# One attention stage of an encoder kernel: score matmuls of two heads interleaved, separate banks for transposed probabilities, rotation split anew over the engines, row factors spread by transposes

## The reference

```python
def rms_norm(x, g):
    x32 = x.astype(jnp.float32)
    y = x32 * lax.rsqrt(jnp.mean(x32 * x32, axis=-1, keepdims=True) + NORM_EPS)
    return (y * g.astype(jnp.float32)).astype(x.dtype)

def apply_rope(x, cos, sin):
    x1, x2 = jnp.split(x, 2, axis=-1)
    return jnp.concatenate([x1 * c - x2 * s, x2 * c + x1 * s], axis=-1)

# mixer of layer 0
q, k, v = jnp.split(h @ w_in, [1024, 1152], axis=-1)      # 16 heads of q, 2 of k, 2 of v
q = apply_rope(q...); k = apply_rope(k...)
logits = einsum('bnqhgd,bnkhd->bnhgqk', qc, kb) * 64 ** -0.5   # chunk n: 64 queries, 128 keys
logits = where(valid, logits, -inf)
probs = softmax(concatenate([logits, sink]))[..., :-1]
out = einsum('bnhgqk,bnkhd->bqhgd', probs, vb) @ w_out
```

## Time and profile before

| what | value |
|---|---|
| median of 3 runs | 1840.58 us (1840.41 to 1841.6) |
| profiled execution | 1839.91 us, span 1838.1 us |
| busy: PE, PEld, DVE, ACT, POOL | 1808.4, 1479.7, 914.1, 623.0, 148.8 us |
| granted TensorE clock, mean | 0.999 |
| first attention, first scores to last transposes | 410.0 to 484.0 us from the span's start |

### The profile page before, as it was taken

How to read it: one execution, slowest core, us unless ns; L and a number is a source line. 1 busy time by engine, 2 the same in 40 slices (tenths; PEclk the granted TensorE clock), 3 DMA queues, 4 the chain that set the end, 5 groups by cost and what they waited for, 6 DMA issues and landing times.

```text
span 1838.1 us, 23399 instructions
## 1 busy us (share of the span) xinstructions
PE 1808.4 (98%) x8601; PEld 1479.7 (80%) x8601; DVE 914.1 (50%) x1407; ACT 623.0 (34%) x1044; POOL 148.8 (8%) x124
## 2 busy tenths in 40 slices
PE   7999999999999999999999999999999999999998
PEld 5888888877788888888888888888766788888886
DVE  5443433468654434335543343456897544344344
ACT  5422222335543223223322222233466442222222
POOL 0100100012101001000110010100000010010010
PEclk9999999999999999999999999999999999999999
DMA  6333333233233333332333333234111333333321
GB/s 173 109 95 99 92 103 89 83 106 84 76 97 95 100 92 102 97 92 86 103 103 94 98 94 103 83 94 113 30 40 58 92 102 101 95 91 103 92 83 55
DMA packets 322097, 169.94 MB, mean 92 GB/s; under 512 B 13362, under 2 KB 317679, under 8 KB 322031
## 3 DMA queue, kind: packets, MB, share of 16 engines
q1 hardware_dynamic: 321680, 168.26, 32.0%
q10 hardware_dynamic: 350, 0.83, 0.1%
HBM read 162.50 MB, written 2.10 MB: 90 GB/s over the span
## 4 chain that ended last, share of the span: by engine, by line
PE 64%; issue 29%; DVE 3%; DMA 2%; POOL 1%; SPq 1%; ACT 0%; POOLq 0%; DVEq 0%; ACTq 0%
PE bank L1077 21%; PE bank L1078 21%; PE bank L1079 21%; POOL work L458 1%; DVE work L934 1%; DMA w_raw<-b_kvup 1%; SPq L388 0%; DMA r_kv<-work 0%; DMA work<-x 0%; PE bank L1195 0%; PE bank L1105 0%; DVE w_lo L710 0%; PE bank L1182 0%; PE bank L1094 0%; DMA m_q<-work 0%
## 5 line engine op out<-in xcount | busy, mean ns | idle before, releaser
L1077 PE MATMUL bank<-h_hi,w_hi 128*128 128x512 f32 x1536 | 601.2, 391 | 1.9 <-issue 1.7
L1079 PE MATMUL bank<-h_hi,w_lo 128*128 128x512 f32 x1536 | 598.3, 390 | 0.0
L1078 PE MATMUL bank<-h_lo,w_hi 128*128 128x512 f32 x1536 | 598.2, 389 | 0.0
L710 DVE TENSOR_TENSOR w_lo<-w_raw,w_hi 128x1024 fp32r<-128x1024 f32 (+2 forms) x320 | 394.4, 1233 | 317.1 <-ACT w_hi L518 309.0
L518 ACT ACTIVATE w_hi<-w_raw 128x1024 fp32r<-128x1024 f32 (+2 forms) x320 | 319.5, 998 | 296.1 <-PE bank L1079 296.0
L1077 PEld LDWEIGHTS bank<-h_hi,w_hi 128*128 128x128 f32 x1536 | 288.8, 188 | 62.3 <-issue 2.2
L1079 PEld LDWEIGHTS bank<-h_hi,w_lo 128*128 128x128 f32 x1536 | 288.6, 188 | 60.3
L1078 PEld LDWEIGHTS bank<-h_lo,w_hi 128*128 128x128 f32 x1536 | 288.9, 188 | 59.1
L1077 PE MATMUL bank<-y_hi,w_hi 128*128 128x512 f32 x832 | 325.1, 391 | 0.9 <-DVE xT L782 0.7
L1079 PE MATMUL bank<-y_hi,w_lo 128*128 128x512 f32 x832 | 323.8, 389 | 0.0
L1078 PE MATMUL bank<-y_lo,w_hi 128*128 128x512 f32 x832 | 323.7, 389 | 0.0
(11 more groups left out here) (136 smaller groups left out, 972.7 us busy)
## 6 DMA issues: line engine op xcount, KB each, us to landing
w_raw<-ffn_gu SPq DMA_DIRECT2D x176, 512.0 KB, 3.8
w_raw<-ffn_d SPq DMA_DIRECT2D x64, 512.0 KB, 3.7
w_raw<-ffn_d SPq DMA_DIRECT2D x32, 384.0 KB, 3.3
w_raw<-a_in SPq DMA_DIRECT2D x10, 512.0 KB, 3.9
w_raw<-a_out SPq DMA_DIRECT2D x8, 512.0 KB, 3.7
w_raw<-b_out SPq DMA_DIRECT2D x8, 512.0 KB, 3.6
w_raw<-b_in SPq DMA_DIRECT2D x5, 512.0 KB, 3.9
w_raw<-b_qup SPq DMA_DIRECT2D x16, 144.0 KB, 2.3
```

Of the source, the lines that this page charges most:

```text
L710: last = v.tensor_tensor(w_lo[:, sl, 0:k, 0:m], w_raw[:, sl, 0:k, 0:m], w_hi[:, sl, 0:k, 0:m].bitcast(F32), ALU.subtract)
L1077: t.matmul(b[:, :], wh, hi[:, c, :], start=c == 0, stop=False)
L1078: t.matmul(b[:, :], wh, lo[:, c, :], start=False, stop=False)
L1079: last = t.matmul(b[:, :], wl, hi[:, c, :], start=False, stop=c == k - 1)
```

## The change

Four things change, three of them in the first attention.

1. `scores_a`: the loop over chunks is outside and the loop over the two heads inside, so that consecutive matmuls address the four 64 by 64 quarters of the array. Both heads' `s_full` come with the last chunk. The transposed probabilities go to banks 5 and 6 (`TA`); the scores wait for the exponentials of the pair before (`exp_done`), and the transposes for ACT's copy of the pair before.
2. The query block is copied from its bank by ACT without scaling (`raw`); the norm's factors are multiplied into the cosine and sine tables once, by DVE. ACT makes this copy between its two copies of transposed probabilities (ahead of everything else at pair 0).
3. From block 2 on, SP issues two of the four exchange DMAs and ACT the other two, after its second copy and before `high`. SP's exchanges from block 2 on stand one weight load earlier. POOL makes only the cosine product; the sum is made by DVE (`rotated`) right after `sine_a`. DVE's `low` comes after the probabilities.
4. `diag` is gone. PE transposes the column of factors, read 128 times over, with the identity: four transposes instead of four products with ones. It waits for the last of the four short steps only.

```diff
@@ sync, exchange
+        def exchange(eng, n, c, parts):
+            eng.wait_ge(evac_done, block_a(n, c) + FIRST + 1)
+            if c >= 2:
+                eng.wait_ge(rot_done, c - 1)
+            for x in parts:
+                y = x ^ 1
+                eng.dma_start(swapped[c % 2][x * ROPE_B:(x + 1) * ROPE_B, :],
+                              raw_a[y * ROPE_B:(y + 1) * ROPE_B, c % 2, :]).then_inc(swap_in[c % 2], 16)
...
-                    sp.wait_ge(sine_done, c - 1)
-                for x in range(4):
...
+                exchange(sp, k_block, c, range(4) if c < 2 else (0, 1))
             for j in range(2, 2 + PAIRS + KD):
+                if 9 <= j < 8 + PAIRS:
+                    swap(j - 7)
                 if j < 2 + PAIRS:
                     load(k_block + j, 0, cols(a_in[0], (j - 2) * P, P))
...
-                elif 8 <= j < 8 + PAIRS:
-                    swap(j - 7)
+                elif j == 8:
+                    swap(1)
@@ gpsimd
                 g.tensor_tensor(dst, raw, cos, ALU.mult).then_inc(t1_done, 1)
+                if c >= 2:
+                    return
...
-            pool.wait_ge(t_in, 32)
+            pool.wait_ge(table_r, 2)
@@ scalar
-            for k in range(3):
-                high(n + k + AHEAD)
+            def raw(c):
+                blk = block_a(n, c)
+                act.wait_ge(pe_done, blk + FIRST + 1)
+                if c >= 2:
+                    act.wait_ge(rot_done, c - 1)
+                a.activation(raw_a[:, c % 2, :], bank[RING[blk][0]][:, :], ACT.Copy).then_inc(evac_done, 1)
+            high(n + AHEAD)
+            raw(0)
+            high(n + 1 + AHEAD)
+            act.wait_ge(evac_done, n + 1 + FIRST + 1)
+            high(n + 2 + AHEAD)
+            raw(1)
             for p in range(PAIRS + 1):
                 if p > 0:
                     for e in range(2):
                         act.wait_ge(t_full, 2 * (p - 1) + e + 1)
-                        a.activation(pt_a[:, e, :], SC[e][:, :], ACT.Copy).then_inc(pt_done, 1)
+                        a.activation(pt_a[:, e, :], TA[e][:, :], ACT.Copy).then_inc(pt_done, 1)
+                        if e == 0 and p + 1 < PAIRS:
+                            raw(2 + p)
+                elif p + 1 < PAIRS:
+                    raw(2 + p)
                 if p + 1 < PAIRS:
+                    exchange(act, n, 2 + p, (2, 3))
                     high(n + 3 + p + AHEAD)
@@ vector
-                if spread:
-                    for i in range(TT):
-                        last = v.tensor_scalar(diag[:, i, :], ident, st[:, 5, i:i + 1], None, ALU.mult)
-                    last.then_inc(diag_ready, 1)
...
-            def scaled_a(c):
...
+            def rotated(c):
+                dve.wait_ge(sine_done, c + 1)
+                dve.wait_ge(t1_done, c + 1)
+                q = qt_a[:, c % 2, :]
+                v.tensor_tensor(q, q, swapped[c % 2][:, :], ALU.add).then_inc(rot_done, 1)
...
+            v.tensor_tensor(cos_a, cos_a, r_x[:, :], ALU.mult).then_inc(table_r, 1)
+            v.tensor_tensor(sin_a, sin_a, r_x[:, :], ALU.mult).then_inc(table_r, 1)
...
-                if p + 1 < PAIRS:
-                    scaled_a(2 + p)
...
                 if p + 1 < PAIRS:
-                    low(n + 3 + p + AHEAD)
                     sine_a(2 + p)
+                    rotated(2 + p)
...
+                if p + 1 < PAIRS:
+                    low(n + 3 + p + AHEAD)
                 if p > 0:
                     pair_out(p - 1)
@@ tensor
-                pe.wait_ge(diag_ready, count["stat"])
+                pe.wait_ge(nstep, 4 * count["stat"])
...
-                    last = t.matmul(MISC[:, i * P:(i + 1) * P], ones[:, :], diag[:, i, :], start=True, stop=True)
+                    last = t.transpose(MISC[:, i * P:(i + 1) * P], st[:, 5, i:i + 1].to_broadcast([P, P]), ident)
...
+                    if p == 0:
+                        pe.wait_ge(v_ready, 1)
+                    else:
+                        pe.wait_ge(pt_done, 2 * (p - 1) + e + 1)
...
-                for e in range(2):
-                    if p > 0:
-                        pe.wait_ge(pt_done, 2 * (p - 1) + e + 1)
-                    rows = slice(e * HD, (e + 1) * HD)
-                    for c in range(NC):
+                if p > 0:
+                    pe.wait_ge(exp_done, 2 * p)
+                for c in range(NC):
+                    for e in range(2):
+                        rows = slice(e * HD, (e + 1) * HD)
```

More of the change, by code:

```diff
@@ L188, in build @@
         r_kv = sb("r_kv", [P, S])
-        diag = sb("diag", [P, TT, P])
         cst = sb("cst", [P, C_END])
@@ L238, in build @@
         VTB = bank[5:7]
+        TA = bank[5:7]
         OB = bank[7]
@@ L266, in build @@
         nstep = sem("nstep")
-        diag_ready = sem("diag_ready")
         silu_done = sem("silu_done")
@@ L274, in build @@
         t1_done = sem("t1_done")
+        table_r = sem("table_r")
         rot_done = sem("rot_done")
@@ L381, in swap @@
             def swap(c):
-                sp.wait_ge(evac_done, block_a(k_block, c) + FIRST + 1)
-                if c >= 2:
-                    sp.wait_ge(sine_done, c - 1)
-                for x in range(4):
-                    y = x ^ 1
-                    sp.dma_start(swapped[c % 2][x * ROPE_B:(x + 1) * ROPE_B, :],
-                                 raw_a[y * ROPE_B:(y + 1) * ROPE_B, c % 2, :]).then_inc(swap_in[c % 2], 16)
+                exchange(sp, k_block, c, range(4) if c < 2 else (0, 1))
             for j in range(2, 2 + PAIRS + KD):
+                if 9 <= j < 8 + PAIRS:
+                    swap(j - 7)
                 if j < 2 + PAIRS:
@@ L744, in refine, with rms_values @@
                 dve.wait_ge(nstep, count["n"])
-            def rms_values(m, width, spread=True, between=None):
+            def rms_values(m, width, between=None):
                 dve.wait_ge(misc_full, m + 1)
@@ L871, in _ @@
             n = ffn(0, 0, G_MIX)
-            def scaled_a(c):
-                b = product(block_a(n, c))
-                if c >= 2:
-                    dve.wait_ge(rot_done, c - 1)
-                v.tensor_tensor(raw_a[:, c % 2, :], b[:, :], r_x[:, :], ALU.mult).then_inc(evac_done, 1)
             def sine_a(c):
+                dve.wait_ge(table_r, 2)
                 dve.wait_ge(swap_in[c % 2], 64 * (c // 2 + 1))
@@ L889, in _ @@
             rms_spread(3, r_x)
-            scaled_a(0)
+            dve.wait_ge(t_in, 32)
+            v.tensor_tensor(cos_a, cos_a, r_x[:, :], ALU.mult).then_inc(table_r, 1)
+            v.tensor_tensor(sin_a, sin_a, r_x[:, :], ALU.mult).then_inc(table_r, 1)
             low(n + 1 + AHEAD)
             b = product(n + 1)
+            dve.wait_ge(evac_done, n + FIRST + 1)
             v.tensor_tensor(vpad[:, CHUNK:CHUNK + S], b[:, :], r_x[:, :], ALU.mult).then_inc(evac_done, 1)
             low(n + 2 + AHEAD)
-            dve.wait_ge(t_in, 32)
-            scaled_a(1)
             sine_a(0)
@@ L1049, in _ @@
             n = ffn(n, M_F, G_FIN, keep=True)
-            rms_values(M_F + 2, D, spread=False)
+            rms_values(M_F + 2, D)
             for i in range(TT):
@@ L1180, in transposes_a @@
                     pe.wait_ge(p_ready, 2 * p + e + 1)
+                    if p == 0:
+                        pe.wait_ge(v_ready, 1)
+                    else:
+                        pe.wait_ge(pt_done, 2 * (p - 1) + e + 1)
                     for i in range(TT):
-                        last = t.transpose(SC[e][:, i * P:(i + 1) * P], p_a[e][:, i * P:(i + 1) * P], ident)
+                        last = t.transpose(TA[e][:, i * P:(i + 1) * P], p_a[e][:, i * P:(i + 1) * P], ident)
                     last.then_inc(t_full, 1)
@@ L1197, in scores_a @@
                                         kpad[rows, p // 4, c * CHUNK:c * CHUNK + P], start=True, stop=True)
-                    last.then_inc(s_full, 1)
+                        if c == NC - 1:
+                            last.then_inc(s_full, 1)
             def outputs_a(p):
```

## The result

The changed kernel takes 1829.03 us, median of 4 runs (1828.47 to 1829.38); the kernel before, in the same session, 1840.49 (1839.73 to 1841.6, 4 runs). The ratio is 0.9937, with a 95% interval of 0.992 to 0.9954. The forecast was 1828.5 us. The profiled execution took 1829.38 us, with a span of 1827.6; before it was 1839.91 and 1838.1, so 10.5 us went where 12.0 were forecast.

What follows compares the result with a forecast made beforehand. PE, busy 98% of the span, was taken as the bound. 8.3 us from the first attention plus 3.7 from the spreads made 12.0 off 1839.9, so 1827.9, and 1828.5 as median; range 1825.4 to 1833.4 us.

Steps and rivals of the forecast that it cites:

- Scores: First attention on PE: interleaved heads cut a pair's scores from 1.78 to 1.10 us, saving 4.5 us in all.
- Rival A: First attention: the scores don't run four at once and keep 1.78 us; 1833.7 us, chance 0.10.
- The loop: DVE and ACT per pair: probabilities in time by 1 us, so PE's 3.9 us of waits for them go.
- A pair above 9 us: First attention: a sign that the prediction is wrong, if a pair stays that long; pairs 2 to 4 expected at 8.7.
- Attention as a sum: First attention: 4.5 us from scores plus 3.9 from waits, less 0.1 in pair 7, gives 8.3 us saved.
- Exchange: First attention: ACT's second DMA lands 2.0 us after issue, 3.9 at worst; 0.95 late, eaten by 1 us of slack.
- rival B: First attention: exchange lands late beside SP's weight load, PE waits 0.45 us in seven pairs; 1831.7 us, chance 0.12.
- ACT's issues: First attention: two exchange issues of 0.59 us each on ACT, hidden; exponentials can't start before T + 2.6 anyway.
- Rival C: First attention: issues hold ACT long, kernel slower from 1.85 us an issue on; 1848.8 us, chance 0.05.
- Spreads: Eight spreads on PE, transposes replacing diagonals: six save 2.5 us, that at 1472 saves 1.2; 3.7 us in all.
- The one at 1270: Spread before a late-landing weight block: its saving counted as 0, bounds 0 and 1.3 us.
- rival D: More gain: the spread at 1270 counts (1.3 us) and the scores take 0.95 us; 1826.2 us, chance 0.08.

Runs made afterwards that it cites:

- e1: The changed kernel with all 8 score matmuls of head 0 ahead of head 1's again, the banks staying apart; 1831.84 us.
- after_again: The changed kernel once more, unaltered, in the session of another group of runs; 1828.32 us, ratio 0.9936.
- e4: The changed kernel with one spread of eight made by diagonals again, the one at 1259 us (1270 before the change); 1828.99 us.
- e5: The changed kernel with the latent query norm's sums moved behind one more block of value products on PE; 1829.07 us.
- e12: The changed kernel with four latent-attention broadcasts issued one weight load later and DVE's low part of attention outputs ahead of the next weight block's; 1825.41 us.
- e10: The changed kernel with SP waiting, from block 2 on, until a block's exchange has landed before issuing the next weight load; 1828.33 us.
- e3: The changed kernel with all spreads by diagonals put back, so that only the attention is changed; 1833.24 us.
- e7: The changed kernel with the rotary sum of query blocks 2 to 7 back on POOL; 1832.34 us.
- after: The changed kernel as first measured and profiled; 1829.03 us, ratio 0.9937.
- e2: The kernel before the change with only the spreads made by transposition, the attention as before; 1837.48 us.
- e6: The changed kernel with SP issuing all four exchange DMAs of a block and ACT none; 1831.81 us.
- e8: The changed kernel with DVE's low part of the next weight block back ahead of the sine product; 1834.87 us.

## Why the prediction was right

**Scores: right, and a little better.** 1.03 us measured, 1.10 taken. Rival A (1.78 stays) is out; e1 shows the order at work.

**The loop: right.** Pairs 2 to 4 took 8.67 us, 8.74 foretold; probabilities at T + 6.1 and T + 7.1 foretold and measured (440.3 and 441.3 with T = 434.18). Apart from 0.11 us in pair 0, PE waits for probabilities only ahead of pair 7 and in it in after_again. In the first profile it also waits 0.66 in pair 5, and that pair took 9.54 us. A pair above 9 us was one of my own signs of being wrong; it came in one pair of this execution and in none of after_again's.

**Attention as a sum.** 8.3 us foretold; A fell by 7.8 in the first profile and by 8.7 in after_again. e4, e5 and e12 have the same 82.3. In after_again the 8.7 are 5.0 from the shorter scores, where I took 4.5 (0.49 in pair 0, 0.75 in each of six pairs), and 3.6 from waits with their restarts, where I took 3.9, and 0.1 ahead of the first scores. The misses of the terms are larger than that of their sum.

**Exchange: the bound failed in one pair.** I took 3.9 us as the worst landing and let the slack of 1 us eat it. ACT's second issue takes 0.87 us, not 0.59, and a landing of 4.4 us came up: 0.87 us lost in pair 5. A late landing that reaches PE is rival B's mechanism, but B had the weight load as its cause and seven pairs as its price. In e10 a landing was late without the load, and the late ones go with a packet of instructions instead.

**ACT's issues: right.** Two take 1.41 us; the exponentials start at T + 2.8 (436.96), 2.6 foretold. ACT's 436.96 row, behind its issues:

```profile
434.48 1.41 ACTq L337 DMA_DIRECT2D r_kv<-work  x2
436.00 1.06 ACT L526 ACTIVATE w_hi<-w_raw 128x1024 fp32r<-128x1024 f32 x1 [1.05 <-issue]
436.96 0.35 ACT L636 ACTIVATE work<-bank,sm 128x128 f32<-128x128 f32 x1
```

Rival C needed an issue of 1.85 us in every pair. In e3 one of 1.76 us was seen, once.

**Spreads: 3.7 foretold.** The six cost 0.35 us instead of 0.81 each (2.7 us against 2.5), the one at 1472 saved 1.26 (1.2 foretold). The one at 1270 saved 1.44 on the spot and lost 1.28 of it in the longer wait (1.58 against 0.30), near the 0 that I had counted; in after_again the wait took only 0.67, so there half of what rival D counted stayed. A term was missing behind it: I had none for what a longer wait can do to the clock. In the first profile it cost 1.35 us (9.94 against 8.59 of after_again behind the sums).

**The sum.** In the first profile 7.8 + 2.7 + 1.3 + 1.4 - 1.3 - 1.35 = 10.6, measured 10.5. Without the two accidents it would be 12.8; in after_again the span fell by 13.2. By ratios, 0.9937 and 0.9936, the change saves 11.6 to 11.8 us: between the spans' 10.5 and 13.2, and 12.0 was forecast. That the forecast median is met within 0.5 us is in part luck. The first profile is that of the slowest of its four runs, after_again's that of the fastest of its five. In the fastest the change saved 1.2 us more than I had summed up, and the two losses that I had put at nothing, the late landing and the clock, took more than that back in the slowest. The median lies between them.

## What to carry to other kernels

Small matmuls gain from their order alone: 32 records of 64 by 64 took 1.52 us head by head (e1) and 1.03 with the four quarters in turn. The step from 1.78 to 1.52 is that of the banks and waits. A saving ahead of a transfer is given back in the transfer's wait; look for what stands ahead of its issue on the same queue (here four broadcasts that nobody needs soon), and move that rather than the work that waits. And slack in a loop is spent by the transfers that land late: a step of 0.4 us that fits into the slack of quiet pairs (e7) came with a median 3.1 us slower by the ratios, though part of that may be the late landings of single executions. Read more than one profile before you explain a microsecond.

## What the runs showed of the hardware

The granted clock can fall behind a wait of 1.2 to 1.8 us on PE, and doesn't always. The stretch behind the query norm's sums took 9.92 to 11.53 us at a granted clock of 0.70 to 0.83 after waits of 1.58, 1.84, 1.42, 1.29 and 1.23 us (after, e2, e6, e7, e8), and 8.58 to 8.60 at 1.00 after waits of 1.50, 0.96, 0.81 and 0.24 (e10, after_again, e1, e4). In e5 the clock stayed at 1.00 too, behind its wait of 1.47 us. Two extremes:

```profile
1280.95:1292.48 11.53, 11.53 (x61) 10.59 (x61) 7.94 (x16) 2.50 (x8) 1.01 (x1) 0.70 0.15 39
```
```profile
1278.83:1287.41 8.58, 8.58 (x60) 7.89 (x61) 7.12 (x15) 2.49 (x8) 1.01 (x1) 1.00 0.19 50
```

The first is e6 after 1.42 us, the second e10 after 1.50 us. So behind a wait of 1.42 us on the bound engine 2.9 us more were lost. The same fall came in the attention. All fourteen profiles wait 1.68 to 1.84 us for the first scores, and the clock fell behind it in two: e1, where it was 0.70 in the stretch shown above after a wait of 1.69 us, and e2. The changed kernel's same 1.69 us left it alone. In e8 it fell behind the 1.5 us wait ahead of pair 7. The fall started 0.5 to 2.5 us after PE had resumed (e6 and e8, at the sums).

A landing of an exchange DMA (64 KB, SBUF to SBUF) took 1.9 to 2.4 us in the attention unless a 16 KB packet of the `instruction` queue was under way; with one it took up to 4.4.

Not every difference between two profiles is the kernel's: the first sums of the kernel, ahead of everything that was edited, start anywhere from 30.0 to 31.8 us in these profiles. Stretches were therefore compared by their length, not by their position.
